# Low parts of x on VectorE in place of GpSimd at five layer norm boundaries, with the second half's statistics moved into the first chunk

## The reference, cut to what matters

```python
for l in range(2):
    x = layer_norm(alpha * x + 0.5 * swiglu_ffn(x, ffn1_wi[l], ffn1_wo[l]), ln_g[l, 0], ln_b[l, 0])
    mix = even_mixer(x, ...) if l % 2 == 0 else odd_mixer(x, ...)
    x = layer_norm(alpha * x + mix, ln_g[l, 1], ln_b[l, 1])
    x = layer_norm(alpha * x + 0.5 * swiglu_ffn(x, ffn2_wi[l], ffn2_wo[l]), ln_g[l, 2], ln_b[l, 2])

def layer_norm(x, g, b):
    mu = jnp.mean(x, -1, keepdims=True)
    var = jnp.mean(jnp.square(x - mu), -1, keepdims=True)
    return (x - mu) * lax.rsqrt(var + LN_EPS) * g + b
```

## Time and profile before

| | us |
|---|---|
| median of 3 runs | 3878.07 (3877.42 to 3883.36) |
| the profiled execution, its own time | 3877.59 |
| span of its instructions | 3875.9 |
| PE busy | 3687.2 (95%) |
| DVE busy | 1718.0 (44%) |
| ACT busy | 1364.2 (35%) |
| POOL busy | 545.8 (14%) |

### The profile page before, as it was taken

The page is one execution under the profiler, slowest core; times in us unless marked ns, Lnnn a source line. Parts: engine busy times, 40 slices in busy tenths (PEclk is TensorE's granted clock), DMA queues, the critical chain, the costliest instruction groups (busy, mean ns, idle before and its releaser), DMA issues. The chain is left out here.

```text
span 3875.9 us, 47706 instructions
## 1 busy us (share of the span) xinstructions
PE 3687.2 (95%) x19042; PEld 3034.2 (78%) x19042; DVE 1718.0 (44%) x2230; ACT 1364.2 (35%) x1881; POOL 545.8 (14%) x477
## 2 busy tenths in 40 slices
PE   8999987999999999887999999999999999999998
PEld 6888865888888888565888888787887887878877
DVE  2224564322432244753422264556663535556643
ACT  2223532422332243422422153345443323444432
POOL 2102102210311030021311021002110010020110
PEclk9999998999999999877999999999999999999999
DMA  3222211222222222000222233222222233231222
GB/s 141 95 87 89 93 55 65 76 93 85 103 87 97 89 100 87 29 1 5 83 97 91 97 117 114 104 76 98 96 93 89 99 123 120 78 118 66 97 87 87
DMA packets 63246, 340.19 MB, mean 88 GB/s; under 512 B 7152, under 2 KB 13696, under 8 KB 33920
## 3 DMA queue, kind: packets, MB, share of 16 engines
q1 hardware_dynamic: 63104, 338.19, 24.5%
HBM read 331.87 MB, written 6.29 MB: 87 GB/s over the span
## 5 line engine op out<-in xcount | busy, mean ns | idle before, releaser
L403 PE MATMUL bank<-x_hi,w_hi 128*128 128x512 f32 (+1 forms) x3328 | 1298.5, 390 | 67.9 <-PEq L450 22.7
L404 PE MATMUL bank<-x_lo,w_hi 128*128 128x512 f32 (+1 forms) x3328 | 1283.9, 386 | 0.0
L405 PE MATMUL bank<-x_hi,w_lo 128*128 128x512 f32 (+1 forms) x3328 | 1283.4, 386 | 0.0
L367 DVE TENSOR_TENSOR w_lo<-raw,w_hi 128x2048 fp32r<-128x2048 f32 (+2 forms) x310 | 652.4, 2105 | 884.0 <-ACT w_hi L362 869.4
L403 PEld LDWEIGHTS bank<-x_hi,w_hi 128*128 128x128 f32 x3328 | 631.6, 190 | 212.7 <-issue 61.2
L362 ACT ACTIVATE w_hi<-raw 128x2048 fp32r<-128x2048 f32 (+2 forms) x301 | 519.8, 1727 | 698.3 <-PE bank L405 694.9
L405 PEld LDWEIGHTS bank<-x_hi,w_lo 128*128 128x128 f32 x3328 | 631.2, 190 | 125.3
L404 PEld LDWEIGHTS bank<-x_lo,w_hi 128*128 128x128 f32 x3328 | 632.2, 190 | 122.5 <-issue 1.0
L403 PE MATMUL bank<-f_g_hi,w_hi 128*128 128x512 f32 (+1 forms) x792 | 292.5, 369 | 0.0
L405 PE MATMUL bank<-f_g_hi,w_lo 128*128 128x512 f32 (+1 forms) x792 | 289.5, 366 | 0.0
L404 PE MATMUL bank<-f_g_lo,w_hi 128*128 128x512 f32 (+1 forms) x792 | 289.5, 366 | 0.0
(11 more groups left out here) (453 smaller groups left out, 4260.8 us busy)
## 6 DMA issues: line engine op xcount, KB each, us to landing
raw<-in_weights SPq DMA_DIRECT2D x222, 1024.0 KB, 4.8
raw<-in_weights SPq DMA_DIRECT2D x96, 704.0 KB, 4.0
raw<-in_weights SPq DMA_DIRECT2D x8, 768.0 KB, 4.1
x_kept<-X SPq DMA_DIRECT2D x2, 2048.0 KB, 13.8
X<-x_kept SPq DMA_DIRECT2D x2, 2048.0 KB, 9.4
work<-in_rpb SPq DMA_DIRECT2D x12, 256.0 KB, 5.1
stats<-in_rpb SPq DMA_DIRECT2D x12, 256.0 KB, 5.2
X<-in_x SPq DMA_DIRECT2D x8, 256.0 KB, 6.0
```

Source lines behind the costliest of these rows:

```text
L367: dve.tensor_tensor(w_lo[:, s, 0:size], raw[:, s, 0:size], w_hi[:, s, 0:size].bitcast(F32), ALU.subtract).then_inc(lo_ready.sem, 1)
L403: pe.matmul(out, wh[:, w], hi(k), start=first and n == 0, stop=False, skip_group_check=not group)
L404: pe.matmul(out, wh[:, w], lo(k), start=False, stop=False, skip_group_check=not group)
L405: mm = pe.matmul(out, wl[:, w], hi(k), start=False, stop=last and n == len(kts) - 1, skip_group_check=not group)
```

## The change

`lead_vector` gets a function `low` with the subtraction that `lead_pool` had, and runs it two tiles behind `scale` (LAG = 2, whose definition moves up), so that the loop over k has ten turns in place of eight. `half_variance` of the second half moves from behind the loop into its turn k = 8, between `low` of tiles 6 and 7. `lead_scalar` does `half_square` of the second half after k = 6 in place of k = 7. `lead_pool` keeps only the two additions of `half_part_sum`. `lead_tensor` does sums and statistics of the second half after k = 4 of the first chunk in place of behind it.

```diff
@@ lead_vector
+            def low(t, k):
+                h = halves[t]
+                dve.wait_ge(rounded.sem, rounded.at(t * KT + k + 1))
+                dve.tensor_tensor(x_lo[:, k, h], X[:, k, h], x_hi[:, k, h].bitcast(F32), ALU.subtract).then_inc(split_ready.sem, 1)
+
+            half_variance(dve, nb, 0)
             for t in range(2):
-                half_variance(dve, nb, t)
                 centre(t, 0)
-                for k in range(KT):
+                for k in range(KT + LAG):
                     if k + 1 < KT:
                         centre(t, k + 1)
                     if k == 0:
                         dve.wait_ge(half_rstd[nb.p].sem, half_rstd[nb.p].at(2 * t + 2))
-                    scale(t, k)
+                    if k < KT:
+                        scale(t, k)
+                    if k >= LAG:
+                        low(t, k - LAG)
+                    if t == 0 and k == KT:
+                        half_variance(dve, nb, 1)
                     if t == 0 and k == 0:
                         half_residual(dve, nb, 1, 0)
                     elif t == 0 and k == 2 and nb.one_early:
@@ lead_scalar
+                        elif k == 6:
+                            half_square(act, nb, 1)
                         elif k == 7:
-                            half_square(act, nb, 1)
                             half_scale(act, nb, 1)
@@ lead_pool
-            for q in range(2 * KT):
-                if q == 2:
-                    half_part_sum(pool, nb, 1)
-                k, t = q % KT, halves[q // KT]
-                pool.wait_ge(rounded.sem, rounded.at(q + 1))
-                pool.tensor_tensor(x_lo[:, k, t], X[:, k, t], x_hi[:, k, t].bitcast(F32),
-                                   ALU.subtract).then_inc(split_ready.sem, 1)
+            half_part_sum(pool, nb, 1)
@@ lead_tensor
-                if t == 0:
-                    half_sums(pe, nb, 1)
-                    half_stats(pe, nb, 1)
+                    if t == 0 and k == 4:
+                        half_sums(pe, nb, 1)
+                        half_stats(pe, nb, 1)
```

More of the change, by code:

```diff
@@ L508, in lead_vector @@
             third_lo(dve, n0 + 2)
+        LAG = 2
         def lead_scalar(act, n0):
@@ L2453, in next_vector @@
             split_lo(dve, n0 + 2 - n0 % 2, 0, n0 % 2, CHUNK)
-        LAG = 2
         def next_scalar(act, work, gain, l, acc, n0):
```

## The result

The changed kernel took 3889.68 us (median of 16 runs, 3882.96 to 3893.86), the kernel before 3879.38 (16 runs, 3873.40 to 3883.36): ratio 1.0025, 95% interval 1.0017 to 1.0033. So it is slower by 7 to 10 us, by more than the 3.8 forecast; the first median lies above the range of 3875.5 to 3887.0, the second inside it.

A forecast was written before the change was run, and what follows sets the result against it. PE is nearly always busy, so only its waits at five boundaries count. Four boundaries at +1.1 us and boundary 1 at -0.6 make +3.8: 3881.4 us profiled, 3881.9 as median, range 3875.5 to 3887.

The forecast's parts named there:

- What bounds the kernel: Whole kernel: PE is busy 3687.2 of 3875.9 us, so only its waits at the five boundaries can change.
- the price of a low part: A low part takes 0.91 us on average on POOL and 0.42 us on DVE.
- DVE's pace: First half of a boundary: DVE alone needs 1.07 us a tile after the change, where PE needs 0.72.
- Boundaries 1, 3, 4, first half: Boundaries with `early_lo`: the second chunk starts 1.1 us later, through late tile 1, DVE's pace and waiting at tile 7.
- Boundaries 2, 5: Boundaries without `early_lo`: PE starts 0.9 us later and the second chunk comes 1.1 us later.
- What boundary 1 gives back: Boundary 1: PE's 1.74 us wait for DVE's convolution shrinks to 0.6, turning +1.1 into -0.6 us.
- Second half hidden: Second half of a boundary: its low parts end before PE wants them, with 2 us of cover.
- The sum, +3.8: Five boundaries together: 4 x 1.1 - 0.6 = +3.8 us, giving 3881.4 us for the profiled execution.
- lower bound, +0.2: Five boundaries together: the least change, if POOL's two additions never meet a DVE operation.
- rival B: Four other boundaries: short bursts lower TensorE's clock, at most 1.7 us lost each, +6.8 more, 3888.7 us; chance 0.1.
- Rival C: Moved statistics do nothing and the pace is hidden, time returning in later waits for DVE: 3878 us; chance 0.2.
- Rival A: Five boundaries: PE's 9.2 us of waits for low parts go, 3868.9 us, or half, 3873.5; chance 0.15, 0.04 in full.

The follow-up runs named there:

- after_again: The changed kernel run again with no edit, for a second profile; 3886.09 us, ratio 1.0018 to the kernel before.
- stats_only: Kernel before with only the second half's statistics moved as in the change, low parts still on POOL; 3887.19 us, ratio 1.0023.
- low_only: Kernel before with only the low parts moved to DVE, statistics where they were; 3882.50 us, ratio 1.0006.
- late_early_lo: Changed kernel with DVE's `early_lo` moved from after k = 2 to k = 8, in front of the second half's variance; 3876.16 us, ratio 0.9991.
- after_warm: Changed kernel plus seven unused small matmuls after tile 0 of the first chunk at boundaries 1, 3 and 4; 3880.84 us, ratio 1.0009.
- late_low7: late_early_lo plus the last first-half low part ahead of the second half's variance and `half_square` after k = 7; 3869.64 us, ratio 0.9976 to the kernel before.
- before_again: The kernel before run again with no edit, as a candidate; 3877.50 us, ratio 0.9999.
- before_late_early: Kernel before with only `early_lo` moved on DVE, from after k = 2 to behind k = 7, low parts still on POOL; 3883.26 us, ratio 1.0011.
- after_shift5: Changed kernel plus five unused matmuls (1.2 us) in the feed forward stage between boundaries 3 and 4; 3883.97 us.
- after_shift10: Changed kernel plus ten unused matmuls (2.5 us) in the feed forward stage between boundaries 3 and 4; mean 3886.2 us.
- before_shift10: Kernel before plus ten unused matmuls (2.5 us) in the feed forward stage between boundaries 3 and 4; mean 3885.6 us.
- before_shift20: Kernel before plus twenty unused matmuls (4.9 us) in the feed forward stage between boundaries 3 and 4; mean 3882.1 us.

## Why the prediction was wrong

**The clock over all runs.** Each execution has its mean granted clock; span times one less that clock is what it lost. The numbers are rounded to 0.001, some 2 us in one run and little in a mean:

```
                  executions   mean us   lost    rest
before            33           3879.0    114.9   3764.1
after             16           3889.0    124.6   3764.3
after_again       11           3885.5    121.5   3764.0
stats_only        11           3886.8    122.6   3764.3
low_only          11           3882.2    115.0   3767.2
late_early_lo     11           3875.6    115.9   3759.8
after_warm        11           3881.5    116.4   3765.1
late_low7         11           3869.2    111.5   3757.7
before_again      11           3878.5    113.1   3765.3
before_late_early 11           3883.2    116.8   3766.4
after_shift5      10           3883.7    123.1   3760.6
after_shift10     10           3886.2    121.6   3764.6
before_shift10    10           3885.6    119.6   3766.0
before_shift20    10           3882.1    114.1   3768.0
```

The standard error of the rest is 0.3 to 0.8 us. What the whole change adds stands in the column of the low clock (114.9 to 121.5 and 124.6, with the rest at 3764.1, 3764.0 and 3764.3), and so it is for stats_only. It is not so in every row: low_only adds 3.1 us to the rest and nothing to the low clock, and after_shift5, with more work, has a rest 3.4 below that of after_again. The columns are not independent, since a slow stretch of PE fills waits that would be there otherwise; at boundary 4, 1.7 us lost appear with +1.8 us in place of 1.1 by order. So how much of the 7 to 10 us the order would cost at the full clock stays open. That the clock carries the excess over the forecast is read from this table. after_warm, which took away nothing but idle time, shows it for single boundaries, 0.9 and 0.6 us at 1 and 3; no run kept the clock up in the whole kernel.

**Step by step.**

- *What bounds the kernel, the price of a low part, DVE's pace.* Right: 0.41 to 0.42 us alone, 1.06 us a tile, both collisions (0.85 and 0.96 us), PE's 1.82 us at tile 1; DVE is busy 16.2 us more, under the 34 set as a bound.
- *Boundaries 1, 3, 4, first half: +1.1.* The chain was right, the wait at tile 7 was 0.30 us. From the first chunk's start to tile 7 were 11.3 us; forecast 10.8. The half us is PE's slower matmuls in between. Result +1.8 at boundary 4. At boundary 3 +0.6, since the kernel before had its low stretch there already.
- *Boundaries 2, 5: +1.1.* Too much: +0.9 and +0.6.
- *What boundary 1 gives back.* The wait for the convolution went (no row for it in the changed kernel), but the low clock took it: -0.1 and +0.1 for -0.6. The sign set for it, a wait "near 0.6", did not fit the -0.6, which needs no wait at all.
- *Second half hidden.* Right: PE has no other wait for a low part there.
- *The sum, +3.8.* Equal to the +3.8 and +3.5 of the profiles by luck: too high at 2 and 5, too low by the clock at 1 and 4. Its lower bound, +0.2, is +0.4 by its own terms (4 x 0.25 - 0.6); nothing hangs on it.
- **The step that failed** is the clock, put at zero in the sum and into rival B with 0.1. "Against it: boundaries 1, 2, 4, 5 have waits up to 1.46 us ... at the full clock" took one profile for a property of the kernel. The sixth boundary's wait of 2.28 us met the low clock in 12 of 14 profiles; the profile that the prediction read was an exception. At boundaries 1, 3 and 4 together the old order had the low clock in 8 of 12 cases over four profiles (and none at 1 and 4 in the two unshifted ones), the changed order in 12 of 12, late_early_lo and late_low7, without the wait at tile 1, in 0 of 6. Rival B's mechanism is what happened, at 1 and 4; its price of 1.7 us was right, though about half is hidden in the waits that follow. The rule of the Trainium skill (TensorE: Matmul & The Clock Gate, HAM oscillation) that I set beside B agrees in kind: waits between bursts bring the clock down, each time anew. The page tells it of waits for DMA that are longer than any wait of PE at these boundaries (1.82 us at most, 2.28 at the sixth), so the fall at these shorter waits is what the runs add.
- *Beyond the boundaries* I had nothing. 4 us of the profiles' difference lay in the odd mixer, where the low clock costs PE 54 to 63 us in every kernel here. It falls otherwise when the stage comes at another time, and 1.2 us of added work take it back. Of the 4 us the time lost at the low clock accounts for 3.4 in the first pair of profiles and 1.7 in the second. Rival C looked for time that returns there, and it went the other way.
- *Rival A* (the waits go) was wrong as it stood, but true of late_low7: DVE makes the low parts in time if `early_lo` and the statistics stand where DVE and ACT are idle.

Open: why the changed order met 438.2 twice in the odd mixer and the other twelve profiles 431.7 to 436.5. Both have the stretch at the lower clock 183 us into the stage; of the others before_shift10 alone has it, with 434.6, so it is not the whole cause. Open too is what sets the even mixer's 255.2 to 264.3 us; the windows show the low clock there and no changed instruction.

## What to carry to other kernels

Price a moved instruction by the tile it stands in front of, not by its own engine's load: 2.2 us of DVE work in front of the second tile of a pipeline cost PE its wait and its clock, and the same instruction in the engine's gap cost PE no wait there (late_early_lo); with POOL at work beside it, it cost POOL's pace again (before_late_early). Where PE waits in short pieces, take more than one profile before calling its clock unchanged, and judge such kernels by many runs with their clock: here a time difference under 5 us can be made by idle matmuls far away. A change that only reorders can be undone part by part; the half that looked free (the statistics) was the dearer one.

## What had not been expected of the hardware

- 1.7 us of meaningless matmuls in a wait made the kernel 5.3 us faster (after_warm, 3880.84 against 3886.09), and 1.2 us of them in full flow did not make it slower (after_shift5, 3883.97). In the profiles the odd mixer alone took 4.7 and 4.1 us less than in after_again.
- 2.5 us of added work cost 7.3 us and 4.9 us cost 2.8 (before_shift10 and before_shift20 against 3878.66).
- The total that PE waited for low parts stayed (9.2 and 9.4 us) while the time lost at the low clock went from 114.9 to 121.5 and 124.6 us.
